# Two fused transformer blocks on one core: the order of the 512- and 256-column products of a K tile

## The reference

```python
# first block: 272 tokens
z = rmsnorm(h) @ w_in                       # 2048 x 6152: q, k, v, gate_b, gate_c, hc, forget
y = concat(forgetting_attention(q, k, v), gate_b * short_conv(gate_c * hc))
h = h + rmsnorm_groups(y) @ w_out           # 2048 x 2048
h = h + (silu(n @ w_gate) * (n @ w_up)) @ w_down   # n = rmsnorm(h); 2048 x 5632 twice, 5632 x 2048
x = rmsnorm(h)[16:]
# second block: 256 tokens
q, k, v, u, gate_attn, gate_pool = split(x @ w_in_2)    # 2048 x 8192
merged = sigmoid(gate_attn) * (attn @ w_branch_attn) + sigmoid(gate_pool) * (pool(u) @ w_branch_pool)
x = layer_norm(alpha * x + merged @ w_out_2)
x = layer_norm(alpha * x + square(relu(x @ w_ff1)) @ w_ff2)   # 2048 x 8192, 8192 x 2048
```

## Time and profile before

| what | value |
|---|---|
| median of 3 runs | 2450.12 us (2449.77 to 2450.78) |
| the profiled execution, its own time | 2449.89 us |
| its span, first to last instruction | 2447.8 us |
| granted TensorE clock, mean | 1.000 |
| PE busy | 2433.8 us (99%), 14762 products |
| PEld busy | 2173.7 us (89%), 14762 loads |
| DVE, ACT, POOL busy | 1614.5, 1202.2, 173.9 us |
| DMA | 449.59 MB, mean 184 GB/s |

### The profile page before, as it was taken

One profiled execution on the slowest core, in us unless ns is written; L12 is line 12 of the kernel. 1 busy time (PEld: TensorE's weight loads), 2 busy tenths in 40 slices (PEclk: granted clock), 3 DMA queues, 4 the chain that ended last, 5 costly groups with the idle time before them and its releaser, 6 DMA issues.

```text
span 2447.8 us, 36417 instructions
## 1 busy us (share of the span) xinstructions
PE 2433.8 (99%) x14762; PEld 2173.7 (89%) x14762; DVE 1614.5 (66%) x2518; ACT 1202.2 (49%) x1728; POOL 173.9 (7%) x195
## 2 busy tenths in 40 slices
PE   8999999999999999999999999999999999999999
PEld 8999998888888888888888888888998888888887
DVE  5646676676666666667677756678885665565667
ACT  6545545544544543455555654544554443443544
POOL 0001111000000000002211102031110000000010
PEclk9999999999999999999999999999999999999999
DMA  7554456666566666665655455565566666656663
GB/s 250 180 161 139 141 165 189 200 184 194 182 198 190 189 190 189 192 190 185 197 188 167 166 185 190 184 193 186 162 196 193 189 189 189 194 190 189 183 193 117
DMA packets 125751, 449.59 MB, mean 184 GB/s; under 512 B 13840, under 2 KB 16400, under 8 KB 125584
## 3 DMA queue, kind: packets, MB, share of 16 engines
q1 hardware_dynamic: 125296, 446.91, 58.8%
q10 hardware_dynamic: 288, 0.36, 0.0%
HBM read 445.12 MB, written 2.10 MB: 183 GB/s over the span
## 4 chain that ended last, share of the span: by engine, by line
PE 96%; DVE 2%; ACT 1%; issue 0%; DMA 0%; ACTq 0%
PE out_bank L614 28%; PE out_bank L618 27%; PE out_bank L615 14%; PE out_bank L617 14%; PE out_bank L622 3%; PE out_bank L621 3%; PE out_bank L623 3%; DVE w_lo L1307 1%; ACT w_hi L895 0%; PE side_bank L734 0%; PE side_bank L694 0%; PE side_bank L749 0%; PE side_bank L725 0%; DVE h L1824 0%; DMA h<-in_tokens 0%
## 5 line engine op out<-in xcount | busy, mean ns | idle before, releaser
L1307 DVE TENSOR_TENSOR w_lo<-raw,w_hi 128x1024 fp32r<-128x1024 f32 x839 | 1037.4, 1240 | 601.0 <-ACT w_hi L895 596.9
L895 ACT CAST w_hi<-raw 128x1024 fp32r<-128x1024 f32 x840 | 878.1, 1049 | 953.6 <-PE out_bank L618 874.8
L614 PE MATMUL out_bank<-a_op,w_hi 128*128 128x512 f32 x1984 | 784.2, 395 | 0.5 <-DVE h L1334 0.3
L618 PE MATMUL out_bank<-a_op,w_hi 128*128 128x512 f32 x1984 | 776.7, 391 | 0.0
L615 PE MATMUL out_bank<-a_op,w_lo 128*128 128x256 f32 x1984 | 558.8, 282 | 0.0
L617 PE MATMUL out_bank<-a_op,w_lo 128*128 128x256 f32 x1984 | 552.0, 278 | 0.0
L617 PEld LDWEIGHTS out_bank<-a_op,w_lo 128*128 128x128 f32 x1984 | 380.1, 192 | 84.3
L615 PEld LDWEIGHTS out_bank<-a_op,w_lo 128*128 128x128 f32 x1984 | 372.9, 188 | 77.0
L614 PE MATMUL out_bank<-b_op,w_hi 128*128 128x512 f32 x992 | 389.7, 393 | 0.0
L618 PE MATMUL out_bank<-b_op,w_hi 128*128 128x512 f32 x992 | 388.0, 391 | 0.0
L614 PEld LDWEIGHTS out_bank<-a_op,w_hi 128*128 128x128 f32 x1984 | 373.1, 188 | 2.0 <-DVE w_lo L1307 0.7
(11 more groups left out here) (302 smaller groups left out, 1974.6 us busy)
## 6 DMA issues: line engine op xcount, KB each, us to landing
raw<-in_w_ff SPq DMA_DIRECT2D x256, 512.0 KB, 4.2
raw<-in_w_in SPq DMA_DIRECT2D x223, 512.0 KB, 3.7
raw<-in_w_gu SPq DMA_DIRECT2D x176, 512.0 KB, 4.2
raw<-in_w_down SPq DMA_DIRECT2D x88, 512.0 KB, 4.3
raw<-in_w_out SPq DMA_DIRECT2D x64, 512.0 KB, 4.3
raw<-in_w_ba SPq DMA_DIRECT2D x16, 512.0 KB, 3.9
raw<-in_w_bp SPq DMA_DIRECT2D x16, 512.0 KB, 3.8
out<-h SPq DMA_DIRECT2D x8, 256.0 KB, 2.3
```

Source lines behind the costliest of these rows:

```text
L614: t_.e.matmul(bank[:, :], wh, a_both, start=start, stop=False, skip_group_check=True)
L618: mm = t_.e.matmul(bank[:, :], wh, a_both, start=False, stop=stop, skip_group_check=True)
L895: a.e.copy(w_hi[:, m % SPLIT, :], raw[:, u % RAW, :]).then_inc(hi_split)
L1307: v_.e.tensor_tensor(w_lo[:, m % SPLIT, :], raw[:, u % RAW, :], w_hi[:, m % SPLIT, :].bitcast(F32), ALU.subtract).then_inc(lo_split)
```

## The change

The condition that picks the order within a K tile of a pair is turned round, with an exception for the first K tile of an output tile. Odd K tiles now do H and then L (lines 614 and 615), even ones L and then H (lines 617 and 618). An output tile's first K tile still does H first, since its first product is the one with `start=True`, which opens the whole bank. Nothing else changes: the same products with the same operands, the same waits at the same places between K tiles, and the signals still at the last product of a step.

```diff
-                        if cols == "pair" and kt % 2 == 0:
+                        if cols == "pair" and (kt % 2 or start):
                             t_.e.matmul(bank[:, :], wh, a_both, start=start, stop=False, skip_group_check=True)
                             mm = t_.e.matmul(bank[:, 0:SEQ], wl, a_hi, start=False, stop=stop, skip_group_check=True)
                         elif cols == "pair":
                             t_.e.matmul(bank[:, 0:SEQ], wl, a_hi, start=False, stop=False, skip_group_check=True)
                             mm = t_.e.matmul(bank[:, :], wh, a_both, start=False, stop=stop, skip_group_check=True)
```

## The result

The changed kernel takes 2472.34 us (median of 3 runs, 2472.22 to 2472.53) against 2450.12 before: 22.2 us more, ratio 1.0091 with a 95% interval of 1.0071 to 1.0111. The forecast was no change, and its range ended at 2453.0. The time is that of the slower rival, 2472, but not for that rival's reason, as the trace shows.

A forecast was written before the change was run, and what follows sets the result against it. The prediction took TensorE, busy in 99% of the span, to bound the kernel through distances between product starts. All terms summed to 0, so it forecast the earlier median, 2450.1 us, range 2447.0 to 2453.0.

The forecast's parts named there:

- the slower rival: At 744 unit starts, a weight load with its wait is exposed behind a 256-column product: 22 us, 2472 us; chance 0.03.
- What bounds the kernel: Whole kernel: TensorE is busy in 99% of the span, so time is the sum of distances between product starts.
- Steps behind a first unit: 2568 steps behind each tile's first unit: same cycle with its cut moved half a step, so 0 us.
- H to H in one bank: Between neighbouring 512-column products in later steps: 0.23 us without a bank change, as with one; price 0.
- L to L across banks: Between neighbouring 256-column products in later steps: 0.12 us with a bank change, judged from 258-column products; price 0.
- The bound of 1 ns a step: 2568 later steps: what the rows can't exclude is about 1 ns a step, 2.6 us either way.
- First units: 408 steps in tiles' first units, H L L H to H L H L: 0, bounds 1.6 us either way.
- Waits: Loads ahead of each unit's first product: 0.08 us of lead still fits behind a 256-column product's 0.12 us; 0.
- Side products, signals and the end: Side products' loads still hide, steps signal at the same time, and the chain's end is unchanged: 0.
- The bank rival: Between 256-column products of 2568 later steps, a bank change saves 4 ns each: 10 us, 2440 us; chance 0.05.

The follow-up runs named there:

- x6: Kernel before the change with only the SBUF places of even and odd K tiles' operands exchanged in the late layout: 2468.09 us, ratio 1.0076.
- sections A to E: Stretches of 150 steps of products alone, old or new order, PSUM bank change moved or absent: old order 693 ns a step, new order with bank change 700.
- x2: Kernel before the change with only each tile's first unit in the order H L H L: 2454.67 us, ratio 1.0019.
- x5: Changed kernel with the SBUF places of even and odd K tiles' operands exchanged in the late layout: 2455.63 us, ratio 1.0024.
- section C: Products alone in the old order H L L H, with the bank change moved between the two 256-column products: 693 ns a step.
- x8: Changed kernel with two more 256-column products ahead of the second step of each pair block's second unit: 2488.19 us, ratio 1.0157.
- sections A, C and E: Products alone in the old order H L L H, bank changing between 512-column products, between 256-column ones, or not at all: 693.3 ns a step.
- F and G: Sections of products alone; the alternating order H L H L of the changed kernel's first units took 700.0 ns a step in a long stream.

## Why the prediction was wrong, step by step

- *What bounds the kernel.* Right: the time is the sum of TensorE's distances, and the loss is exactly there.
- *Steps behind a first unit: 0.* This is the step that failed. Its inference was that "the extra belongs to each product with its weight load, whatever its width and its neighbour, and an order can't save or add any". The extra measured 53 ns a step before and 60 after (700 - 640). It depends on where the moving operands of neighbouring products begin in SBUF and on the state that the stream is in, which no row of the prediction could price one by one. I treated the new stream as the old cycle with its cut moved. In sizes it is; in operands it isn't, since the L pair now goes from the odd operand to the even one, and x6, which exchanges the operands' places and nothing else, shows that this alone costs 18.5 us. The two neighbours that I did price, H to H in one bank and L to L across banks, were priced rightly at 0: banks don't matter (sections A to E). But the row behind the second was misread. The products from 1716.23 to 1716.35 in the earlier trace rows lie on both sides of a K tile of one output tile (24 products a unit, six a tile, and the unit's first product starts at 1715.99), so they share a bank; the bank changes after the sixth product, below, also in 0.12 us. And one in six of the neighbours in the earlier trace rows changes the bank, not a third. That 0 came out right there was partly luck.

```profile
1716.59 0.28 PE L623 MATMUL out_bank<-b_op,w_lo 128*128 128x258 f32 x1
1716.70 0.28 PE L621 MATMUL out_bank<-b_op,w_hi 128*128 128x258 f32 x1
```

- *The bound of 1 ns a step.* It came from the precision of the rows and not from the uncertainty of the transfer to another order. The true term was 6.7 ns, 17 us. That the earlier trace rows agreed with the earlier trace rows to 2 ns in another layout looked like a law; in other layouts the same order costs 693 to 713 ns.
- *First units: -1.6 to +1.6 us.* Also too narrow. They cost 4.8 us alone (x2), about 7 us in the changed kernel by their 710 ns. The 4 ns by which the weight loads' rows differ priced neither.
- *Waits: 0.* The term came out right, but the row under it doesn't say so. The load at 87.00 did let its product start at 87.08, but the next one starts at 87.34, 262 ns on instead of 230: the 0.08 us of lead cost 0.03 us, one product later, and the stream was at 700 ns a step afterwards. So a load as late as that is not free; it is the only one in the pair blocks of the kernel before, behind the start of the first, and the changed kernel has none. In the changed kernel a wait behind an L shows nowhere: ten steps with their unit starts are even, and x5, with every wait behind an L, is 2455.6. So the rival of exposed loads, whose 22 us happen to match the result, was wrong; the loss has a different mechanism than its price.
- *Side products, signals and the end: 0.* Nothing in the runs contradicts it. Behind a side product an L takes 0.20 us to the next start in the changed kernel (213.34 to 213.54 us), 0.12 and the 0.08 that an H had on top before, as the prediction had it. By themselves these terms weren't tried.
- *The bank rival, 2440.* Wrong in sign and in mechanism: section C.

What stays open: the mechanism inside TensorE's reads. The runs show that the start columns of operands and the history of the stream set a step to 693, 700, 707 or 710 ns. They don't show what is rounded, what the state consists of, or why the pair of x8 turns it one way from one state and the other way from the other.

## What to carry to other kernels

On a kernel that is 99% one engine, reordering "equal" work is not free by symmetry: take the distance over hundreds of steps before and after, and price the new order in a stream of products alone, behind more than one entry, before trusting a sum of single distances. Where float32r operands lie packed, try their start columns too, for either order: here the best and worst of 16 cases differ by 20 ns in 693. A rival whose price fits the result isn't thereby right; ask whether the loss lies at its place (unit starts) or everywhere.

## What the hardware showed that I had not expected

- Most steps of four products took whole multiples of 6.67 ns, the time of 16 columns at 2.4 GHz: 693.3 is 104 of them (1536 columns are 96), 700.0 is 105, 706.7 is 106. 703.4, 704.4 and 710.0 occur too.
- The same order and layout ran at 693 or at 700 ns a step depending on what came before, stayed there for 150 steps and more, and was moved by a single pair of 256-column products. In the kernel before, a weight load that came 0.15 us later than usual (at 87.00 us) was followed by a change from 693 to 700 ns a step in the flat layout.
- A change of PSUM bank cost nothing between two 512-column products or two 256-column ones (693.3 in sections A, C and E), nor from a 256- to a 512-column one (700.0 in F and G). A wait on the load behind a 256-column product cost nothing where what it waited for was there (x5).
- Within the stream `L0 L1` of 256-column products the distances alternate, some 117 and 123 ns (240.0 for both): single distances aren't a property of one product.
